# Two wide expert places of a routed SwiGLU in three reduced-precision passes, with the low parts written over the loaded weights

## What is computed

```python
for e in range(N_EXPERTS):            # 8 experts, D_FF_EXPERT = 3584
    out = out + combine[:, e:e + 1] * swiglu(xt, w_gate[e], w_up[e], w_down[e])
def swiglu(x, w_gate, w_up, w_down):
    return (jax.nn.silu(x @ w_gate) * (x @ w_up)) @ w_down
```

## Time and profile before

| | |
|---|---|
| median of 3 runs | 1410.12 us (1407.42 to 1413.28) |
| profiled execution | 1409.12 us |
| its span | 1407.3 us |
| PE busy | 1335.0 us, 95% |
| DVE, ACT busy | 458.1 us and 265.8 us |
| all DMA | 423.49 MB, mean 301 GB/s |

### The profile page before, as it was taken

The page is one execution under the profiler, slowest core; times in us unless marked ns, Lnnn a source line. Parts: engine busy times, 40 slices in busy tenths (PEclk is TensorE's granted clock), DMA queues, the critical chain, the costliest instruction groups (busy, mean ns, idle before and its releaser), DMA issues.

```text
span 1407.3 us, 18535 instructions
## 1 busy us (share of the span) xinstructions
PE 1335.0 (95%) x7760; PEld 747.7 (53%) x7760; DVE 458.1 (33%) x1023; ACT 265.8 (19%) x491; POOL 98.8 (7%) x115
## 2 busy tenths in 40 slices
PE   6989999999999999999997898799999999999996
PEld 5856599999784665454443233254445444333332
DVE  7898865555589650040100010000101000100002
ACT  2551444443254210000000000011000001101101
POOL 4430100000551000000000000000000000000000
PEclk9999999999999999999999999999999999999998
DMA  9433355537121249999999999999596999999993
GB/s 303 144 127 120 108 193 180 180 120 266 64 90 62 105 173 422 416 412 417 421 422 420 423 422 420 420 410 407 240 418 278 375 418 416 417 417 416 417 424 135
DMA packets 106253, 423.49 MB, mean 301 GB/s; under 512 B 21632, under 2 KB 23864, under 8 KB 97976
## 3 DMA queue, kind: packets, MB, share of 16 engines
q1 hardware_dynamic: 100984, 421.75, 75.1%
q10 hardware_dynamic: 5184, 0.52, 0.4%
HBM read 421.20 MB, written 1.05 MB: 300 GB/s over the span
## 4 chain that ended last, share of the span: by engine, by line
PE 76%; DMA 12%; DVE 8%; issue 1%; SPq 1%; ACT 1%; POOL 0%; DVEq 0%; ACTq 0%
PE psall L2435 14%; DMA m_ring<-in_moe_w_down_dram 9%; PE psall L2579 9%; PE psall L2469 8%; PE psall L2550 5%; PE psall L2134 4%; PE psall L2488 4%; PE psall L2450 4%; PE psall L2233 3%; PE psall L2350 3%; PE psall L2352 3%; PE psall L2351 3%; DMA m_ring<-in_moe_w_up_dram 2%; PE psall L2299 2%; PE psall L2590 2%; PE psall L2406 2%
## 5 line engine op out<-in xcount | busy, mean ns | idle before, releaser
L2469 PE MATMUL psall<-m_ring,xeT 128*64 128x448 f32 (+1 forms) x1280 | 201.1, 544 | 11.1 <-DMA m_ring<-in_moe_w_up_dram 6.0
L2435 PE MATMUL psall<-m_ring,xeT 128*128 128x448 f32 x512 | 195.8, 543 | 0.0
L2005 DVE TENSOR_TENSOR hid<-e_silu,psall 128x448 f32<-128x448 f32 x28 | 17.4, 621 | 448.4 <-PE psall L2435 251.4
L2435 PEld LDWEIGHTS psall<-m_ring,xeT 128*128 128x128 f32 x512 | 97.4, 192 | 93.3 <-issue 92.9
L2469 PEld LDWEIGHTS psall<-m_ring,xeT 128*64 128x64 f32 (+1 forms) x1280 | 68.2, 126 | 137.3 <-issue 103.1
L2579 PE MATMUL psall<-m_ring,hidT 128*128 128x512 f32 (+1 forms) x336 | 125.0, 597 | 3.1 <-DMA m_ring<-in_moe_w_down_dram 3.1
L2550 PE MATMUL psall<-m_ring,hidT 128*32 128x256 f32 (+1 forms) x784 | 107.1, 496 | 18.2 <-DMA m_ring<-in_moe_w_down_dram 18.2
L1675 DVE TENSOR_TENSOR w_lo<-ring,w_hi 128x1024 fp32r<-128x1024 f32 x66 | 80.4, 1224 | 67.8 <-ACT w_hi L1266 67.7
L2350 PE MATMUL psall<-hnT_hi,w_hi 128*128 128x256 f32 x352 | 99.7, 283 | 0.7 <-DVE hnT_lo L1813 0.7
L2352 PE MATMUL psall<-hnT_hi,w_lo 128*128 128x256 f32 x352 | 99.5, 283 | 0.0
L2351 PE MATMUL psall<-hnT_lo,w_hi 128*128 128x256 f32 x352 | 98.9, 281 | 0.0
(11 more groups left out here) (341 smaller groups left out, 1482.8 us busy)
## 6 DMA issues: line engine op xcount, KB each, us to landing
m_ring<-in_moe_w_gate_dram SPq DMA_DIRECT2D x128, 896.0 KB, 22.2
m_ring<-in_moe_w_up_dram SPq DMA_DIRECT2D x128, 896.0 KB, 20.4
m_ring<-in_moe_w_down_dram SPq DMA_DIRECT2D x64, 1792.0 KB, 22.8
ring<-in_w_in_dram SPq DMA_DIRECT2D x10, 2048.0 KB, 12.4
ring<-in_ffn_w_gate_dram SPq DMA_DIRECT2D x5, 2048.0 KB, 10.4
ring<-in_ffn_w_up_dram SPq DMA_DIRECT2D x5, 2048.0 KB, 7.7
ring<-in_ffn_w_down_dram SPq DMA_DIRECT2D x5, 2048.0 KB, 7.9
ring<-in_w_out_dram SPq DMA_DIRECT2D x4, 2048.0 KB, 8.0
```

Of the source, the lines that this page charges most:

```text
L2435: ins = M(m_bank(key)[:, 0:MH], x[:, i, 0:P], weights(kind, i, s), start=(i == 0), stop=(i == KT - 1))
L2469: ins = M(m_bank(key)[q:q + shape[0], 0:MH], x[:, i, 0:shape[0]], w[:, m * MW + s * MH:m * MW + (s + 1) * MH], start=(i == 0), stop=(i == ...
```

## The change

Only places A and B are changed, and the ring.

- **Three passes.** A wide chunk is cut in 24 parts: 16 of 896 columns (gate and up, one for each block of 128 rows) and 8 of the down rows (ROWS; six of 1024 columns and two of 512). For each part ACT copies the loaded weights to float32r in `part_hi`, a ring of AHEAD = 4 parts, DVE subtracts that copy from the loaded weights and writes the low part over them in `m_ring`, and PE makes three float32r products for each half. Tokens (`xe_hi`, `xe_lo`) and hidden rows (`hidT_hi`, `hidT_low`) are split in the same way.
- **Order of B.** The 32 tokens need the weights as loaded, so `quad` goes ahead of `wide`, its part of `down` ahead of the wide one, and a low part waits for the event of the quad that reads the same weights ("qh", "w", "qd"). B's loads alternate between gate and up.
- **Giving back.** Units of a wide place are given back one by one, as the part that ends in them is done.
- **The ring** has 16 units. The routing's small tiles move to other memory, and `second_tiles` (small DVE operations) goes from the first pair to the second.

```diff
-MSLOT = 18
+MSLOT = 16
+AHEAD = 4
+ROWS = [(r, 0, 2) for r in range(3)] + [(3, 0, 1), (3, 1, 1)] + [(r, 0, 2) for r in range(4, MB)]
...
+            if 32 in shape:
+                for h in range(UH - 1):
+                    self.event(("qh", it, c, h))
+                self.add(("w", it, c), "V", self.misc())
+                for q in range(2):
+                    self.quiet(("ws", it, c, q))
             for kind, who in (("g", "A"), ("u", "V")):
...
+                for i in range(KT):
+                    self.part((it, c, kind, i))
+                    if i < KT - 1:
+                        self.event(("p", it, c, kind, i))
+                    else:
+                        for q in range(2):
+                            self.add((kind, it, c, q), who, self.rolling())
+                    self.part_done.append(self.n)
+            order = [(kind, h) for kind in "gu" for h in range(UH)]
+            if 32 in shape:
+                order.sort(key=lambda a: a[1])
+            for kind, h in order:
+                self.load(it, c, kind, h, ("p", it, c, kind, UK * h + 1) if h < UH - 1 else (kind, it, c, 1))
...
+        if self.wide(it):
+            if 32 in self.shape(it):
+                self.event(("qd", it, c))
+            for j in range(len(ROWS)):
+                self.part((it, c, "d", j))
+                if keys and j == len(ROWS) - 1:
+                    for key in keys:
+                        self.add(key, "A", key[2])
+                else:
+                    self.event(("dp", it, c, j))
+                self.part_done.append(self.n)
+            self.load(it, c, "d", 0, ("dp", it, c, 3))
+            self.load(it, c, "d", 1, keys[-1] if keys else ("dp", it, c, len(ROWS) - 1))
             return
...
+            def high(upto):
+                while highs[0] < upto:
+                    n = highs[0]
+                    unit_wait(act, *part_unit(n))
+                    if n >= AHEAD:
+                        act.wait_ge(m_ready, experts.part_done[n - AHEAD])
+                    nc.scalar.activation(part_hi[:, n % AHEAD, 0:part_cols(n)[1]], part_raw(n),
+                                         ACT.Copy).then_inc(part_high, 1)
+                    highs[0] += 1
...
+            def wide_silus(it, c, first):
+                high(first + AHEAD)
+                if 32 in experts.shape(it):
+                    m_arrived(act, ("w", it, c))
+                    b = m_bank(("w", it, c))
+                    for s in range(2):
+                        nc.scalar.activation(e_silu[64 * s + 32:64 * s + 64, 2, :], b[64 * s:64 * s + 32, 0:MH],
+                                             ACT.Silu).then_inc(a_silu, 1)
+                high(first + KT + AHEAD)
+                for s in range(2):
+                    m_arrived(act, ("g", it, c, s))
+                    nc.scalar.activation(e_silu[:, s, :], m_bank(("g", it, c, s))[:, 0:MH],
+                                         ACT.Silu).then_inc(m_drained["A"], 1)
...
-            for p, pos, it, c in experts.steps:
-                silus(it, c)
+            high(AHEAD)
+            tokens_high(0)
+            for n, (p, pos, it, c) in enumerate(experts.steps):
+                first, mine, then, further = experts.first_part[2 * n:2 * n + 4]
+                if experts.wide(it):
+                    wide_silus(it, c, first)
+                else:
+                    high(min(first + AHEAD, then))
+                    silus(it, c)
+                high(then)
+                high(min(then + AHEAD, further))
                 if pos == 0 and p:
                     y_out(it - 1)
                 if pos == FIRST_DONE[p]:
                     y_out(2 * p)
                 if pos == PICKS_AT[p]:
                     picks_out(p)
...
+            lows = [0]
+            def low(upto):
+                while lows[0] < upto:
+                    n = lows[0]
+                    it, c, kind, i = experts.parts[n]
+                    dve.wait_ge(part_high, n + 1)
+                    if 32 in experts.shape(it):
+                        if kind == "d":
+                            dve.wait_ge(m_ready, experts.free[("qd", it, c)])
+                        elif i // UK < UH - 1:
+                            dve.wait_ge(m_ready, experts.free[("qh", it, c, i // UK)])
+                        else:
+                            m_arrived(dve, ("w", it, c))
+                    V.tensor_tensor(part_raw(n, True), part_raw(n),
+                                    part_hi[:, n % AHEAD, 0:part_cols(n)[1]].bitcast(F32),
+                                    ALU.subtract).then_inc(part_low, 1)
+                    lows[0] += 1
+            def hidden_low(it, c):
+                for j, (base, rows, r0, r1) in enumerate(experts.r_pieces(it)):
+                    if not base:
+                        m_silu(dve, ("th", it, c, j))
+                        V.tensor_tensor(hidT_low[j][:, :, :], v3(m_bank(("tr", it, c, j))[:, 0:(r1 - r0) * rows], r1 - r0),
+                                        hidT_hi[:, r0:r1, 0:P].bitcast(F32), ALU.subtract).then_inc(m_drained["V"], 1)
+            def quad_hidden(it, c):
+                b = m_bank(("w", it, c))
+                for s in range(2):
+                    m_silu(dve, ("ws", it, c, s))
+                    q = slice(64 * s + 32, 64 * s + 64)
+                    ins = V.tensor_tensor(hid2[0:32, s * MH:(s + 1) * MH], e_silu[q, 2, :], b[q, 0:MH], ALU.mult)
...
-            for p, pos, it, c in experts.steps:
+            for n, (p, pos, it, c) in enumerate(experts.steps):
+                first, mine, then, further = experts.first_part[2 * n:2 * n + 4]
+                if experts.wide(it):
+                    low(first + AHEAD)
+                    if 32 in experts.shape(it):
+                        quad_hidden(it, c)
+                    low(mine)
+                low(min(mine + AHEAD, then))
                 hidden(it, c)
+                low(then)
                 if pos == 0:
                     take_tokens(2 * p + 1)
                 if pos == 1 and p:
                     for j in range(4):
                         add_out(p - 1, j)
-                if pos == 2 and p == 0:
+                if pos == 2 and p == 1:
                     second_tiles()
                 if pos == 2 and p == 1:
                     dve.wait_ge(s_gfin, 16)
...
+                    if experts.wide(2 * p + 2):
+                        tokens_low(2 * p + 2)
+                if len(experts.shape(it)) > 1 and experts.wide(it):
+                    hidden_low(it, c)
+                low(min(then + AHEAD, further))
+                if experts.shape(it) == (P,):
+                    hidden_low(it, c)
...
                 def wide(kind):
                     for i in range(KT):
...
+                        n = experts.part_no[(it, c, kind, i)]
+                        if c == 0 and kind == "g":
+                            for j, (k0, k1) in enumerate(experts.k_pieces(it)):
+                                if i == k0:
+                                    pe.wait_ge(xe_low, xe_count(it, j))
+                        pe.wait_ge(part_low, n + 1)
+                        lo = part_raw(n, True)
                         for s in range(2):
                             key = (kind, it, c, s)
                             if i == 0:
                                 m_open(pe, key, k)
-                            ins = M(m_bank(key)[:, 0:MH], x[:, i, 0:P], weights(kind, i, s), start=(i == 0),
-                                    stop=(i == KT - 1))
-                            if i == KT - 1:
+                            y = m_bank(key)[:, 0:MH]
+                            cols = slice(s * MH, (s + 1) * MH)
+                            hi = part_hi[:, n % AHEAD, cols]
+                            M(y, xe_hi[:, i, :], hi, start=(i == 0), stop=False)
+                            M(y, xe_lo[:, i, 0:P], hi, start=False, stop=False)
+                            ins = M(y, xe_hi[:, i, :], lo[:, cols], start=False, stop=(i == KT - 1))
+                            if i == KT - 1 or s:
                                 event(ins)
-                        if i % UK == UK - 1 and i < KT - 1:
-                            event(ins)

...
                 elif shape[0] == P:
+                    if 32 in shape:
+                        for h in range(UH):
+                            for kind in "gu":
+                                unit_wait(pe, it, c, kind, h, k)
+                            ins = quad(h)
+                            if h < UH - 1:
+                                event(ins)
                     for kind in "gu":
                         wide(kind)
-                    if 32 in shape:
-                        for h in range(UH):
-                            quad(h)
                 else:
...
+            def wide_down(it, c):
+                m_wait_drained(pe, ("tr", it, c, 1))
+                last = c == experts.chunks(it) - 1
```

(27 more changed lines are left out.)

108 lines of the change are left out of this document (85 added, 23 removed).

## The result

Before: 1409.0 us median (1406.5 to 1414.5, 20 executions). After: 1413.8 (1407.7 to 1420.9, 20 executions). The ratio is 1.0031, with a 95% interval of 1.0016 to 1.0045: 4.4 us more, 2.3 to 6.3. It lies inside the forecast's range (1392 to 1422) and inside what it called no change, but beyond its interval on the other side of 1 from the forecast.

The account below looks back on a forecast made before the run. Transfers bound the routed layer, with 30 us of stops to win. Transfers ending 6.8 us earlier, less 1.9 for one clock fall, gave -5: 1409.12 to 1404, or 1405 as median; range 1392 to 1422.

Parts of the forecast that it names:

- what it called no change: Whole kernel: a time within 7 us of before, some 0.5%, given a chance of 0.38.
- What bounds the kernel: Routed layer: bound by transfers near 417 GB/s; only 30 us of stops in the third pair, B's, can be won.
- The rest of the kernel follows the transfers: After the third pair: transfers end 6.8 us earlier and all later work moves with them.
- The first pair never stops DMA: Place A: chunks cost PE over 26.4 us, but E's 24 units take it 12.16 and 6.04 against 53.
- Passes and feeding: Wide chunks: parts at 1.20 us, copies 0.96 and subtractions 1.15 hidden, 7.6 us less per chunk if nothing waits.
- The borders: Between phases of a chunk: waits of 1.3 us gate to up, 1.85 or 2.95 quad to down; transposes 3.4.
- The tally of PE: Third pair: start differences summed from B's first chunk, 4.2 us later, to C, 7.5 us earlier at 1162.2.
- one fall of 1.9: New waits: one more drop of the granted clock, costing 1.9 us beyond the tally.
- The tally of the ring: Third pair, 16 units: stops of 21.3 us in place of 30, 104.5 units at C, transfers ending 6.8 us earlier.
- the last full moment of the ring: Third pair: at 1134.8 us with 92 units, then 12.5 more units until C.
- The clock: Third pair: falls of 1.9 us at twelve border waits, 1426 if all; 0.23 together with border waits at upper bounds.
- the borders at their bounds: Third pair: border waits at their upper bounds, C starting at +7.6, 1418; 0.23 together with the clock rival.

Follow-up runs that it names:

- Kernel 5: The changed kernel with ScalarE making gate's silus before the fourth look-ahead copy of up, transposed rows left in place: 0.9993 of the kernel before.
- kernel 4: The changed kernel with ScalarE making gate's silus and copying the transposed rows before the fourth look-ahead copies: 0.9973 of the kernel before.
- kernel 8: As 7, and ScalarE copies the transposed rows before any look-ahead copy where a chunk of B comes next: 0.9976 of the kernel before.
- 7: On top of kernel 4, TensorE makes the two passes on the high parts before waiting for the low part: 0.9988 of the kernel before.
- kernel 9: The changed kernel with unread products filling TensorE's idle time inside B's transposes, cut to size, and before B's first quad: 1.0019 of the kernel before.
- kernel 1: The kernel before with a ring of 16 units in place of 18, nothing else changed: 1.0051 of the kernel before, 7.2 us more.
- kernel 3: The changed kernel with place B in one full pass as before, A in three passes, ring of 16: 1.0052 of the kernel before.
- kernel 2: The changed kernel with place A in one full pass as before, B in three passes, ring of 16: 1.0016 of the kernel before.
- kernel 11: Kernel 8 with fillings of the right size and 7 products before the last pair's early scatter: 0.9948 of the kernel before, 1403.6 us median.

## Why the prediction was wrong, step by step

**What bounds the kernel** held up to the last load. In a stretch without stops the transfers move 415 to 422 GB/s in all traces, and what changes is how long they stand. "The rest of the kernel follows the transfers" did not hold: 3.3 of the 7.7 us between the two traces lie behind them, in the slower scatter and last down, and the forecast had nothing for that. The clock falls there in other kernels too (ring alone: 5.15 and 14.05 us in place of 3.67 and 13.89).

**"The first pair never stops DMA"** failed, with little weight. It was argued from sums (A's chunk against 26.4 us, E's 24 units against 53), and sums don't show when a ring is full. 16 units are just too few there: 2.8 us lost with the ring alone, 1 in most traces of the changed code, 5.3 in the one where the clock fell in A's first chunk.

**Passes and feeding** held. Parts come 1.21 us apart, copies take 0.95 us and subtractions 1.09 (896 columns), both hidden. Where subtractions follow each other, four take 4.10 us. The Trainium skill, "VectorE: DVE Perf Modes", section "The DRAIN you can't avoid", would have each wait some 0.8 us for the one before, by an estimate from that page, but also says that an operation which nothing holds starts earlier; these rows show no such wait.

**The borders** were right in place and nearly in price: gate to up waits 1.06 us (forecast 1.3), behind quad 1.42 (1.2), transposes take 3.1 to 3.7 us with their own work (3.4). But the forecast took them as the price of the change, and the dearest of them was only the order of one queue: ScalarE made a fourth copy before the silu, and that copy could not begin before the last part of gate was done. Kernel 5 moves it and takes 5.4 us back.

**"The tally of PE"** is the step that failed: the third pair takes 256.5 us where it had 247.4. Reckoned as the forecast did, from the landing of the units of D at 911.12 (now 914.12), it is 260.1 against 251.1 to C's start, 9.0 us too long. By the tally's own steps, measured less forecast, read from PE's timeline: to B's first part +0.6; the four phases of parts, 20.9 to 21.0 us in place of 20.5, together +1.9 (the same phase without the border wait is 19.9 and not 19.2); from B's first chunk to its second quad +1.1, since the last down of D takes 13.6 us again, which I had put down to its units and which is the clock (12.2 in kernels 4 and 8); the quads of the second and fourth chunk, 7.4 and 7.8 in place of 6.15, +3.0; E's first gate and up +1.6; the down behind E's second gate and up, and on to C, +1.4; the other steps together -0.5. That is the 9.0 but for rounding. 5.7 of it are the clock (1.1, 3.0 and 1.6), where the forecast took one fall of 1.9, and that on its end sum. The slow first quad, 9.28 us, costs nothing: its end is bound by the landing of its units, and B's first part comes 16.1 us behind the down of D in after as in kernels 4 and 8. (The tally's C has a slip of 0.2 in it: E's start at -7.4 and E's down at +0.1 give -7.3 and not -7.5.) With 3.0 us before the third pair, 9.0 in it and 3.3 at the end, less the 1.9 that were allowed, the forecast of -5 becomes about +8, and the traces differ by 7.7.

**"The tally of the ring"** charged the two missing units their 4.4 us. Alone they cost 7.2 us (3.9 to 10.4), of which 2.8 lie in the first pair. The end of its chain held better: the kernels whose third pair has the length of the forecast (4, 7 and 8: 247.1 to 247.9) are 1.7 to 3.8 us faster than before, and -5 had been forecast for it. What it left out are PE's waits for units, 1 to 3 us in quad's share of down there: the last full moment of the ring is one constraint, and PE coming too early for its units is the other.

**The clock** was the rival with 0.23 (with the borders at their bounds). Its mechanism is there and its price is not. In windows of after:

```profile
925.00:930.00 5.00, 5.00 (x32) 1.50 (x28) 2.02 (x2) 0.00 (x0) 0.00 (x0) 0.50 1.04 414
...
975.00:980.00 5.00, 5.00 (x39) 2.00 (x42) 1.27 (x3) 0.36 (x1) 0.00 (x0) 0.66 1.01 420
1025.00:1030.00 5.00, 5.00 (x35) 2.12 (x39) 0.25 (x1) 0.36 (x1) 0.00 (x0) 0.66 0.67 238
```

The clock goes to its lower level of 1.2 GHz (0.50, or 0.66 on average of a window) and back: behind the wait before the first quad, in the last down of D, and behind three of B's four transposes. None of the waits between gate and up or quad and down has a fall of its own behind it. The Trainium skill, "TensorE: Matmul & The Clock Gate", section "A second HAM failure mode: psum-queue depth-cycling", has such swings behind brief, frequent idling; the trace agrees for three of the twelve waits that the rival counted and not for the other nine. The fall in the last down of D is no price of the change: the trace of before has it too, 13.59 us, and its cause is open. And kernel 9, whose trace has none of the three behind the transposes, is 1.7 us faster than after and not the 4.6 that they took from quads and E. Between executions of one kernel the clock goes with most of the spread: over 82 of before 0.9 us for each 0.001 of the mean clock, over the 20 of after 1.1. Across kernels it does not: ring 16 has before's clock and 7.2 us more, kernel 4 has 0.980 against before's 0.988 and is 3.8 us faster.

So the 4.4 us are +7.2 for the ring (shown by kernel 1), 0 for A's passes (kernel 3 against 1), and about -3 for B's passes with quad first (after against 1; kernel 2 against 1 has -5; all these intervals overlap, but the two kernels with one pass in B, taken together, are clear of the two with three). B's passes make PE's third pair no shorter than one pass does, 256.5 us in both at 16 units. The 30 us that the matmuls save go into the border waits, the slower clock and B's first chunk, where quad waits for eight units: its gate, up and quad end 37.1 us behind the down of D, where they ended 31.3 behind it. What the order of ScalarE's queue and the filled waits could give back, 12 us, kernel 11 shows.

Two things stay open: why kernel 11 is 4 us faster than kernel 8 at the same length of the third pair, and what brings the clock down in one execution and not in the next, at the end of the kernel above all.

## What to carry to other kernels

When a change pays for its buffers with slots of the ring that hides the transfers, price the slots alone first: run the old kernel with the smaller ring. Here two units of eighteen cost more than the whole change, and the next two, in the changed kernel, three times as much. And when an engine is given look-ahead work, put what another engine waits for ahead of the last copy: that copy can't start before the same event, and what stands behind it is late by its full length.

## What the runs showed of the hardware that I had not expected

A wait of 1.6 us of TensorE behind a short group of transposes was enough for the next 64 matmuls to take 7.4 us in place of 6.2; with ten matmuls of no use in 1.5 us of that wait they took 6.2. One trace does not prove the filling, since kernels have the same falls in one execution and not in another: kernels 4 and 7 have the same four waits at the transposes, and only the trace of 7 shows falls behind the first and the last. The mean clock over 12 executions, 0.984 with the fillings and 0.978 without, does speak for it. Of the 20 executions of after, the seven with a mean clock of 0.976 or below took 1416.9 us on average, the five at 0.980 or above 1409.7. One trace of such a kernel is not enough to charge a stop to the change, as the one at 556 us shows.
